# Experts visited in order of their token counts, in passes of 64 or 32 slots

## What is computed

```python
def _hier_moe(u, p):
    ...
    for e in range(N_EXPERTS):                       # 32, in the second block 16
        h = jax.nn.silu(t @ p['w_exp_gate'][e]) * (t @ p['w_exp_up'][e])
        y = y + combine[:, e:e + 1] * (h @ p['w_exp_down'][e])
```

## Time and profile before

| | us |
|---|---|
| median of 3 runs | 1474.62 (1473.76 to 1475.71) |
| span of the profiled execution | 1474.6 |
| PE busy (matmuls) | 1431.9 (97%) |
| DVE busy | 605.8 (41%) |
| ACT busy | 224.1 (15%) |
| moved by DMA | 435.48 MB, 295 GB/s over the span |

### The profile page before, as it was taken

The page is one execution under the profiler, slowest core; times in us unless marked ns, Lnnn a source line. Parts: engine busy times, 40 slices in busy tenths (PEclk is TensorE's granted clock), DMA queues, the critical chain, the costliest instruction groups (busy, mean ns, idle before and its releaser), DMA issues.

```text
span 1474.6 us, 19938 instructions
## 1 busy us (share of the span) xinstructions
PE 1431.9 (97%) x8514; PEld 986.2 (67%) x8514; DVE 605.8 (41%) x1228; ACT 224.1 (15%) x430; POOL 18.0 (1%) x44
## 2 busy tenths in 40 slices
PE   9999999999999999999999998989999999999996
PEld 7888888688888886555455444446788876455542
DVE  1557998989963252222221211115123251211222
ACT  0220100411112023110111010102122022111011
POOL 0000000000000000001000000000010000000000
PEclk9999999999999999999999999999999999999999
DMA  9731223864343768999999999995654658999975
GB/s 382 319 120 58 101 85 120 351 235 177 117 171 139 326 277 326 385 426 416 426 425 428 428 428 427 426 427 220 191 217 162 258 232 323 427 427 427 426 308 247
DMA packets 37198, 435.48 MB, mean 295 GB/s; under 512 B 4449, under 2 KB 5865, under 8 KB 10873
## 3 DMA queue, kind: packets, MB, share of 16 engines
q1 hardware_dynamic: 34272, 427.89, 71.2%
q0 software_dynamic: 1664, 4.52, 0.9%
q10 hardware_dynamic: 1176, 1.84, 0.8%
HBM read 431.61 MB, written 2.62 MB: 294 GB/s over the span
## 4 chain that ended last, share of the span: by engine, by line
PE 84%; DMA 13%; DVE 1%; ACT 0%; issue 0%; SPq 0%; POOL 0%; ACTq 0%; DVEq 0%; POOLq 0%
PE PP L880 21%; PE PP L1221 18%; PE PP L1236 9%; PE MB L1010 7%; DMA ZC<-in_w_moe 6%; PE MB L1205 5%; DMA KQ<-in_w_moe 5%; PE PP L1034 3%; PE MB L1008 3%; PE PP L918 3%; DMA RA<-in_w_moe 2%; PE PP L950 2%; PE PP L1197 1%; PE MB L1060 1%; PE PP L868 1%; PE MB L950 1%
## 5 line engine op out<-in xcount | busy, mean ns | idle before, releaser
L880 PE MATMUL PP<-uT,ring 128*128 128x256 f32 x704 | 153.2, 379 | 0.0
L880 PEld LDWEIGHTS PP<-uT,ring 128*128 128x128 f32 x704 | 133.4, 190 | 18.5 <-issue 0.5
L1947 DVE TENSOR_SCALAR wctx<-wctx 128x1 f32<-128x1 f32 x50 | 7.7, 154 | 304.4 <-PE PP L1221 304.4
L1494 DVE SCALAR_TENSOR_TENSOR ZC<-ZC,vec 128x256 f32<-128x256 f32 x240 | 116.2, 484 | 7.8
L1221 PE MATMUL PP<-ring,const 128*64 128x256 f32 x992 | 112.4, 380 | 5.5 <-DMA ring<-in_w_moe 4.8
L1205 PE MATMUL MB<-V 64*128 64x512 f32 x400 | 112.1, 639 | 1.7 <-DVE V L1970 0.9
L1221 PEld LDWEIGHTS PP<-ring,const 128*64 128x64 f32 x992 | 71.8, 137 | 48.6 <-issue 9.0
L1962 DVE SCALAR_TENSOR_TENSOR V<-V,wctx 128x256 f32<-128x256 f32 x100 | 48.5, 485 | 114.7 <-PE MB L1205 100.0
L740 ACT ACTIVATE V<-PP 128x256 f32<-128x256 f32 x50 | 19.2, 384 | 376.4 <-PE PP L1221 376.4
L1236 PE MATMUL PP<-ring,const 128*64 128x512 f32 x320 | 73.1, 598 | 0.6 <-ACT const L748 0.6
L1221 PE MATMUL PP<-ZC,const 128*64 128x256 f32 x512 | 59.9, 388 | 4.9 <-DMA ZC<-in_w_moe 4.6
(11 more groups left out here) (477 smaller groups left out, 2034.2 us busy)
## 6 DMA issues: line engine op xcount, KB each, us to landing
ring<-in_w_moe SPq DMA_DIRECT2D x53, 2048.0 KB, 17.4
RA<-in_w_moe SPq DMA_DIRECT2D x20, 2048.0 KB, 14.3
ZC<-in_w_moe SPq DMA_DIRECT2D x20, 2048.0 KB, 16.2
Vc<-in_w_moe SPq DMA_DIRECT2D x17, 2048.0 KB, 17.5
KQ<-in_w_moe SPq DMA_DIRECT2D x17, 2048.0 KB, 19.5
extra<-in_w_moe SPq DMA_DIRECT2D x17, 1792.0 KB, 15.1
ring<-in_w_ada SPq DMA_DIRECT2D x12, 2048.0 KB, 10.6
ring<-in_w_gates SPq DMA_DIRECT2D x7, 2048.0 KB, 7.8
```

The source lines that it names most:

```text
L880: ins = pe.matmul(out[:, c, :], W[:, k * width + at:k * width + at + P], X[:, k, :], start=k == 0, stop=k == K - 1)
L1494: ins = V_.scalar_tensor_tensor(conv[:, t, :], zpad[:, t, k:k + L], tap, conv[:, t, :], ALU.mult, ALU.add)
```

## The change

Both stages sort the experts on DVE by count, with experts 0, 1 and 2 kept at the front (their weights are asked for before the counts are known). A position in this order, not an expert, owns a pass: `expert_passes` fixes the size of each position's pass, 64 or 32 slots. In stage 0 positions 0 to 17 have 64 slots and 18 to 29 have 32; position 30 is the loop's first round and position 31 is visited only if it has tokens. In stage 1 positions 3 and 4 have two passes (64 and 32) over one set of weights, 5 to 8 have 64, 9 to 14 have 32, large and small alternate, and position 15 is the loop's first round. Rounds of the loop are 32 slots. From the tenth transfer on SP reads the expert's number from the table for each. A pass of 32 runs gate and up interleaved, in four quarters of the array, and down and the scatter in four quarters as well. The output's banks are now one for each 256 columns, both token halves in one, and the scatter of a 64-slot pass is four matmuls of 256 columns for each token half instead of two of 512.

```diff
+def expert_passes(n):
+    E = EXPERTS[n]
+    if n == 0:
+        order = list(range(E - 2))
+        sizes = {p: (64,) if p < LEAD + 15 else (32,) for p in order}
+    else:
+        order = list(range(LEAD)) + [LEAD + r for r in (0, 6, 1, 7, 2, 8, 3, 9, 4, 10, 5, 11)]
+        sizes = {p: (64, 32) if LEAD <= p < LEAD + 2 else (64,) if p < LEAD + 6 else (32,) for p in order}
...
+            def load_expert(n, w):
+                x, s = loads[w], a[f"w_moe{n}"]
+                p, q, bay = x["pos"], x["q"], bays[x["bay"]]
+                e = sp.value_load(tab[0:1, p:p + 1], min_val=0, max_val=EXPERTS[n] - 1)
+                sp.wait_ge(job_done, last_of[x["prev"]] + 1)
...
+                sp.dma_start(bay, s[bass.ds(3 * e + q, 1)].rearrange("a p n -> p (a n)")).then_inc(w_full[x["bay"]], 16)
...
                 with sp.Fori(0, T) as i:
-                    e = sp.value_load(tab[0:1, bass.ds(i + 72, 1)], min_val=0, max_val=E - 1)
+                    p = sp.value_load(tab[0:1, bass.ds(i + TAB_ITEM, 1)], min_val=0, max_val=E - 1)
+                    e = sp.value_load(tab[0:1, bass.ds(p, 1)], min_val=0, max_val=E - 1)
...
+                def scatter(t, size, done=None, first=False):
+                    for q in (0, 2, 1, 3) if size == 64 else (0, 1, 2, 3):
+                        g, at = (q // 2, L * (q % 2)) if size == 64 else (q, 0)
+                        rows = slice(size * g, size * (g + 1))
+                        ins = pe.matmul(MB[q][:, t, :], S[rows, t * P:(t + 1) * P], ys[rows, at:at + L], start=first and t == 0,
+                                        stop=done == "acc_done", tile_position=(size * g, 0))
...
+                def gate_and_up(Wg, Wu, x, done):
+                    for k in range(DT):
+                        for q, (W, first) in enumerate(((Wg, 2), (Wu, 0))):
+                            for g in range(2):
+                                at = 32 * (first + g)
+                                ins = pe.matmul(bank[0][at:at + 32, 0:L], x[:, k, 0:32], weights(W, k * 512 + g * 256, 256),
+                                                start=k == 0, stop=k == DT - 1, tile_position=(0, at))
+                            if k == DT - 1:
+                                ins.then_inc(done[q], 1)
...
+                def down(k, W, size):
                     pe.wait_ge(m["ht_ready"], k + 1)
+                    G_, width = P // size, D * size // P
                     for c in range(4):
-                        for g in range(2):
...
+                        for g in range(G_):
+                            ins = pe.matmul(bank[2][size * g:size * (g + 1), 0:width],
+                                            hts[:, c % 2, size * (c // 2):size * (c // 2 + 1)],
+                                            weights(W, c * D + g * width, width), start=c == 0, stop=c == 3,
+                                            tile_position=(0, size * g))
...
+                gather_rows(0)
+                link(V_.scalar_tensor_tensor(key, e_("cnt"), 1024.0, e_("off"), ALU.mult, ALU.add))
+                link(V_.tensor_tensor(key[:, 0:LEAD], key[:, 0:LEAD], cst("boost", LEAD), ALU.add))
+                for r in range(E // 8):
+                    left, best = work if r else key, srt[:, 8 * r:8 * r + 8]
+                    link(V_.max(best, left))
+                    ins = V_.max_index(order[:, 8 * r:8 * r + 8], best, left)
+                    if r < E // 8 - 1:
+                        link(V_.match_replace(work, best, left, -1e9))
+                say(dve, ins, m["routed"], 2 * n + 1)
+                of_tokens(r_("tokkey"), key.unsqueeze(1).unsqueeze(1).to_broadcast([P, 2, LT, E]))
+                for c in range(1, 4):
+                    gather_rows(c)
...
+                for c in range(1, 8):
+                    link(V_.scalar_tensor_tensor(work, level, 32.0 * c, work, ALU.is_gt, ALU.add))
...
+                sizes = [one["size"] for one in PASSES[n]]
+                job_wait(dve, J[f"moe{n}", 1, 0])
+                hidden(0, sizes[0], 64)
...
-                for t in range(LT):
-                    for g in range(2):
-                        dve.wait_ge(m["acc_done"], 2 * t + g + 1)
-                        ins = V_.bn_stats(bst[:, t, 6 * g:6 * g + 6], acc[t][g])
+                for q in range(4):
+                    dve.wait_ge(m["acc_done"], q + 1)
+                    for t in range(LT):
+                        ins = V_.bn_stats(bst[:, t, 6 * q:6 * q + 6], MB[q][:, t, :])
```

More of the change, by code:

```diff
@@ L86 @@
 FIRST_MOE0 = (2, 0, 1, 3, 8, 5, 7, 4, 6)
+def expert_passes(n):
[6 more added lines that the diff above has]
+        sizes = {p: (64, 32) if LEAD <= p < LEAD + 2 else (64,) if p < LEAD + 6 else (32,) for p in order}
+    passes, base, caps, code = [], [0] * E, [0] * E, 0
+    for slot, p in enumerate(order):
+        base[p], caps[p] = code, sum(sizes[p])
+        for part, size in enumerate(sizes[p]):
+            passes.append(dict(slot=slot, pos=p, size=size, second=part > 0, base=code))
+            code += size
+    inline = max(order) + 1
+    base[inline], caps[inline] = code, 32
+    for p in range(inline + 1, E):
+        base[p] = code
+    assert passes[-1]["size"] == 32 and passes[0]["size"] == 64
+    return order, passes, base, caps, code
+ORDER, PASSES, BASES, CAPS, LOOP_CODE = zip(*(expert_passes(n) for n in range(2)))
 def make_jobs():
@@ L106, in experts @@
     def experts(n):
-        for e in range(EXPERTS[n] - 1):
+        first = len(loads)
+        for slot, p in enumerate(ORDER[n]):
             for q in range(3):
-                jobs.append(dict(src=f"moe{n}", b=3 * e + q, kind="moe", half=0, w=len(loads), i=len(jobs)))
-                loads.append(dict(src=f"moe{n}", b=3 * e + q, bay=bay_of(f"moe{n}")))
+                loads.append(dict(src=f"moe{n}", b=3 * p + q, bay=bay_of(f"moe{n}"), pos=p, q=q))
+        for k, one in enumerate(PASSES[n]):
+            for q in range(3):
+                jobs.append(dict(src=f"moe{n}", b=3 * k + q, kind="moe", half=0, w=first + 3 * one["slot"] + q, i=len(jobs)))
     order = (("mix1", (("ada", 4, ["ada"]), ("piece", PIECES, []), ("glu", 4, ["cm8"]), ("q", 2, ["cm8"]),
@@ L264, in build @@
         spread = (bank[3], flat(MB[2]))
-        acc = [[flat(MB[2 * t + g]) for g in range(2)] for t in range(LT)]
         yt_pair = 1 - J["u2", 0, 0]["pair"]
@@ L507, in _ @@
                 load(w)
-            for w in range(at[0] + len(FIRST_MOE0), at[1]):
-                load(w)
+            sp.wait_ge(moe[0]["routed"], 1)
+            for w in range(at[0] + 3 * LEAD, at[1]):
+                load_expert(0, w)
             last_experts(0)
@@ L512, in _ @@
                 load(w)
-            for w in range(at[2], at[3]):
-                bay = loads[w]["bay"] if w <= at[2] + SPARE else None
+            for w in range(at[2], at[2] + 3 * LEAD):
+                bay = loads[w]["bay"]
                 if bay == 7:
@@ new lines, in route @@
+                link(V_.tensor_tensor_scan(e_("xinc"), e_("zero"), work, 0.0, ALU.max, ALU.add))
+                link(V_.tensor_tensor(e_("xfirst"), e_("xinc"), work, ALU.subtract))
+                dve.wait_ge(b2["ld"], 16 * 14 if n else 16)
+                cap_off, base_off, adj = (by_pos[n][:, E * v:E * (v + 1)] for v in range(3))
+                V_.tensor_tensor(base_off, base_off, off_at, ALU.subtract)
+                V_.scalar_tensor_tensor(adj, e_("xfirst"), 32.0, adj, ALU.mult, ALU.add)
@@ new lines, in linked, with hidden @@
+                def linked(ins, k, step):
+                    ins.then_inc(m["step"], 1)
+                    dve.wait_ge(m["step"], k * 3 + step)
+                def hidden(k, size, before):
+                    linked(V_.tensor_scalar(slotcols, slotcols, float(before), None, ALU.add), k, 1)
+                    dve.wait_ge(m["sg_ready"], k + 1)
+                    if size == 64:
+                        V_.tensor_tensor(hid, bank[1][:, 0:L], sg, ALU.mult).then_inc(m["hid_ready"], 1)
+                    else:
+                        V_.tensor_tensor(hid[0:64], bank[0][0:64, 0:L], sg[0:64], ALU.mult).then_inc(m["hid_ready"], 1)
@@ L2177, in constants @@
     put("eps", np.broadcast_to(np.array([LN_EPS, RMS_EPS]), (P, 2)))
-    put("slot", np.concatenate([np.broadcast_to(np.arange(P), (P, P)), (p % SLOTS - SLOTS)[:, None]], axis=1))
+    put("slot", np.concatenate([np.broadcast_to(np.arange(P), (P, P)), (p % 64 - 64)[:, None], (p % 32 - 64)[:, None]], axis=1))
+    put("boost", np.broadcast_to(BOOST * (LEAD - np.arange(LEAD)), (P, LEAD)))
+    for s in range(2):
+        lift = np.where(np.arange(EXPERTS[s]) < LEAD, BOOST / 1024 * (LEAD - np.arange(EXPERTS[s])), 0.0)
+        put(f"caps{s}", np.broadcast_to(lift + np.array(CAPS[s]), (P, EXPERTS[s])))
     return c
@@ L2228, in layout @@
     d["const"] = constants()
+    for n in range(2):
+        caps, bases = np.array(CAPS[n]), np.array(BASES[n])
```

(1 more changed line is left out.)

359 lines of the change are left out of this document (206 added, 153 removed).

## The result

The changed kernel takes **1460.61 us** (median of 4 runs, 1459.66 to 1462.72), the kernel before beside it 1474.36. The ratio is 0.9903 with a 95% interval of 0.9889 to 0.9917: 13.8 us faster, where 20.1 were forecast. The profiled execution has a span of 1460.7 us and took 1462.72 in all. In every run on record that gives both, the time is about 1.8 us or more above the span.

A forecast was written before the change was run, and what follows sets the result against it. Stage 0 bound by transfers in its second half; stage 1 by PE first, by the loop's transfers at its end. 1474.6 - 9.9 (stage 0) - 11.4 (stage 1) + 1.2 (ends) = 1454.5 us; range 1446 to 1470, own range 1449 to 1461.

The forecast's parts named there:

- Part 1: Both stages' fetches: stage 0 drops one 14.7 us fetch; stage 1 goes from 18 fetches to 17, 3 rounds to 2.
- Part 2: Small pass: four quarters run at once, gate and up 3.45 us, down 1.8, whole pass 7.7, or 8.4 with residual.
- Part 3, the clock: Gate and up behind idle PE: half clock level expected, +1.75 us each, bounds 0 and 3.45.
- the +1.75: Extra us for each gate and up after an idle stretch, from stage 0's last up product: 5.36 instead of 3.6.
- Part 4: Stage 0's first pass: product behind sort and longer list ends at 563.3, PE stalls, +3 us, bounds 0 and 6.
- The rest of the kernel is not touched.: Code outside the two stages: left out of the sum, apart from the stages' ends at plus 1.2 us.
- A: Rival on small passes: quarters cost more than columns, gate and up 5.4 us, down 2.7; time 1470; chance 0.15.
- B: Rival on small passes: quarters run two at a time, gate and up 6.9 us, pass 12.9; time 1490; chance 0.07.
- the chain of 2.5 us: Small pass, between gate-and-up and down: silu, product, turn, copy and wake-ups, uncovered; 2.5 us, or 3.2 with residual.
- C: Rival: clock stays up (7 us) or first pass's stall is covered (3); 1444.5 at best; chance 0.13 for below 1449.
- the stall: PE's wait in stage 0's first pass, 560.64 to about 563.5, moving the transfers' end by +3 us.
- D: Rival: boosted front or ties leave stage 1's rounds as before; one more fetch and round, 13 us, 1467; chance 0.02.

The follow-up runs named there:

- e_large: Changed kernel with 64 slots at stage 0's positions 0 to 28, 32 only at 29 and in the loop: 1461.62 us, ratio 0.9911.
- e_bays: Changed kernel with stage 0's third use of the spare bay dropped, which shifts the order of bays behind it: 1455.07 us, ratio 0.9851.
- e_second: Changed kernel with a second pass of 32 slots for position 2 in stage 1, over the same weights; one loop round instead of two: 1450.75 us.
- the profile beside the table: First profile of the changed kernel, no edit; span 1460.7 us, the execution took 1462.72 us.
- the second profile: Profile of the changed kernel run again with no edit, beside the experiments; median 1460.24 us, ratio 0.9895.
- b_relb: Kernel before, with the table of relative biases written 16 instead of 128 times a head: 1476.21 us beside 1475.21, ratio 1.0005.
- e_fill_more: Changed kernel with unread filler products in PE's waits: 22 ahead of late small passes, 48 in stage 0's loop, 30 in stage 1's: 1453.96 us.
- e_stall: Changed kernel with stage 0's first product of gate and up computed by DVE in the middle of the loop's list, not behind it: 1457.59 us.
- e_relb: Changed kernel with the table of relative biases written 16 instead of 128 times a head, read back by eight transfers of 16 partitions: 1457.28 us.
- e_pairs: Changed kernel with all gate products ahead of all up products in a small pass, two quarters at a time: 1467.35 us, ratio 0.9955.
- e_fill: Changed kernel with unread filler products in PE's waits: 18 ahead of late small passes and stage 1's loop rounds, 36 in stage 0's: 1459.94 us.

## Why the prediction was right, and where it was not

**Part 1, what is fetched: right, and its times in part by luck.** One round less in each stage, 50 passes, and the loops' requests came where the working had them. Stage 0's at 975.84 (975.4 forecast), with the up weights at 988.36 (988.1). Stage 1's last at 1426.21 (1429.8 less the 3.9 by which the stage began earlier: 1425.9), up weights at 1438.63 (1438.6). But in stage 0 the 30th pass's weights came 1.0 earlier than forecast and its gate and up took 1.2 to 1.4 longer, and the two cancel. In stage 1 the working had the queue idle between 1304.4 and 1312.2 (3.9 taken off), behind position 4's two passes. The trace has it full there (DMA share 1.01 over 1300 to 1308) and half idle before, over 1260 to 1280 (0.55), while position 3's second pass held its gate weights until 1273.3, which the working passed over. e_large shows that the eleven small passes give stage 0 next to nothing, e_bays what its empty queue gives back, and e_second that a fetch is worth far more than a pass.

**Part 2, the small pass: right.** Gate and up 3.5 to 3.6 (3.45), down 1.9 (1.8), a small pass with residual 8.3 and 7.9 (8.4). The short matmuls of the earlier trace rows were a fair guide: the four quarters do run at once, and that they stream two weight tiles costs nothing. The Trainium skill ("TensorE: Matmul & The Clock Gate", Part 3, measured speedup) has 3.07 times for four row tiles. The trace doesn't agree for this form: four column quarters, 32 streams of 256 columns in 3.5 us against 6.9 for as many in halves, are half, so all four ran at the full rate. A large pass got no slower by its scatter (12.99 us, as before); I had 0.2.

**Part 3, the clock: right in kind, too small.** This is the mis-sized term inside the stages. I took the +1.75 of the one disturbed product before for every wait. Measured above 3.5 us, in the profile beside the table: +3.0 ahead of stage 0's loop, +2.9 in it, +1.7 and +3.0 in stage 1's rounds, 10.7 in all where 7.0 were taken. In the second profile the same four give +1.7, +2.1, +1.6 and +3.0, 8.4 in all. So the sign is shown and the size is not fixed: one row was too little for it, and b_relb's profile has the same product undisturbed (3.67), behind a wait of 1.23 us. The row before began 2.3 us after the last product, at the full level, and was at half for about 3 us; these began 5 to 10 us after, and the worst stayed at half almost to their end. e_fill_more is the evidence that it was the clock and not the transfers or the quarters: behind waits for the same transfers, with PE kept busy, the three rounds take 3.7 us.

**Part 4, the first pass: right, 2 us and not 3.** DVE's product ended at 562.79 (563.3), PE's turn came at 562.84 instead of 560.6, and the next gate product 2.1 us later than before. The removal gives it back (e_stall: stage 0 ends 3.0 us earlier than in the second profile).

**The step that failed** is one sentence: "The rest of the kernel is not touched." Its code isn't, but its work moved 8.3 us earlier, against a transfer that did not follow. The table's round trip ended at about 1082.4 before (the last read asked for at 1079.6, 2.8 us to landing) and was wanted at 1085.0: 2.6 us of slack, which I had not looked for. In the changed kernel it is sent 8.3 us earlier, and its last read still lands at 1082.3. The write took 45.9 us instead of 42.7 (45.3 to 47.1 in every profile of the changed kernel that has it), and the last read needed 7.8 us instead of 2.8. The times fit a collision that the longer write brought about: the reads are now asked for at 1070.8 to 1074.5, across SP's request for 2 MiB at 1072.1, where before all of them (1075.8 to 1079.6) came ahead of it (1080.4). That is an argument from the two timelines. Neither the collision nor why the write itself is slower was tried. That the round trip is the cause of the loss is shown by e_relb, and by b_relb that it was none before. The write's length goes with its bytes: 1.5 MB in 46 us, an eighth of it in 7. One page bears on it: by the Trainium skill ("DMA: Bandwidth & Descriptors", "Why a DMA increments its semaphore by 16 and not by 1") a transfer is spread over the largest number of engines, up to 16, that divides the slowest dimension of both its sides, here the 8 heads. No run here shows which engines worked.

**The rivals.** A is out for the quarters, and B is out as a state of the change. e_pairs also shows that B's price for gate and up was too high: in pairs, with all gate products first, the time is 1467, not 1490. I had left the chain of 2.5 us as it was, where the up product covers a part of it, and had let every small pass count, where many have a transfer behind them. Whether B as it was written would have been slower than before stays open, since it also had down at 3.6 us, which e_pairs leaves at 1.9. C had the stall about right and the clock wrong way round. D did not occur.

The range of 1446 to 1470 held the time; the forecast's own range, 1449 to 1461, held it at its edge. By the profile beside the table, which is of the slowest of the four runs, the sum was 6.2 us too low: 4.4 for the phase between the stages, and 2.0 for the two stages together, where the clock cost 3.7 more than taken over its four waits, the stall 0.9 less and the rest 0.8 less. By the second profile (span 1458.4) it was 3.9 too low: 2.3 between the stages and 1.6 in them and at the ends.

## What to carry to other kernels

When a stage gets shorter, look at what runs beside it on another clock: list each long transfer that spans the stages, with the time at which it lands and the time at which its data are wanted. If it lands no earlier than before, only that slack of the gain gets past the place that waits for it (here 2.6 of 8.3 us). Count a fetch and a pass apart: here one fetch less for the same number of passes was worth 9.5 us, and halving eleven passes that wait for transfers was worth next to nothing. A loop that reuses its bays asks too late twice, ahead of its first round and between rounds; a different rotation of bays, at no cost, gave 5.2 us.

## What was not expected of the hardware

- A small pass that waits for a transfer pays twice, since the clock falls too. After 2.59 and 3.22 us idle (e_fill, 1418.04 and 987.61) it was still at the full level at the restart and fell within 0.7 us; after 2.87 (e_fill, 968.67) and 3.50 (e_fill_more, 969.96) it did not fall at all, and gate and up behind at most 1.5 us of waiting stayed at the full level every time. After 4.61 us (at 938.53 in the changed kernel) it also began at the full level and fell within 0.9 us. So the length of the wait alone does not give the price: in the changed kernel's two profiles gate and up behind a wait of 4 us or more took 5.0 to 6.6 us, against 3.5.
- Four quarters of 32 columns with two different streamed tiles ran fully at once: 64 records of the trace in 3.48 to 3.66 us, in pairs 6.1 to 6.2.
- A 1.5 MB write of 8 partitions to memory ran at 34 GB/s (1,572,864 bytes in 45.65 us) and did not speed up when all queues together moved only 108 (1030 to 1050).
